# Weight sums of the last stage's fourteen Strassen tiles: from VectorE to GpSimd

## The reference

```python
y = jax.nn.gelu(y).astype(h.dtype)
y = y * jax.nn.sigmoid(y @ w_glu + b_glu)              # w_glu 2048 x 2048
...
xa = memory_attention(xq, mem_n, xa_w_kv[i])           # 4 heads, 256 memory tokens
y = jnp.concatenate([seq_out, xa], axis=-1) * jax.nn.silu(z)
x = x + y @ w_out[i]                                   # w_out 3072 x 1024
return rms_norm_2(x, final_norm_w)
```

## Time and profile before

| | |
|---|---|
| median of 3 runs | 1545.64 us (1544.82 to 1546.47) |
| profiled execution, its own time | 1545.65 us |
| its span, first to last instruction | 1543.7 us |
| mean granted TensorE clock | 0.994 |
| busy: TensorE, VectorE, ScalarE, GpSimd | 97%, 44%, 19%, 12% |
| the last stage | 1345.1 to 1543.7 us of the span |
| GpSimd in the last stage | 2.08 us busy |

### The profile page before, as it was taken

The page is one execution under the profiler, slowest core; times in us unless marked ns, Lnnn a source line. Parts: engine busy times, 40 slices in busy tenths (PEclk is TensorE's granted clock), DMA queues, the critical chain, the costliest instruction groups (busy, mean ns, idle before and its releaser), DMA issues. The chain is left out here.

```text
span 1543.7 us, 22762 instructions
## 1 busy us (share of the span) xinstructions
PE 1496.5 (97%) x9125; PEld 987.0 (64%) x9125; DVE 680.3 (44%) x1313; ACT 293.9 (19%) x559; POOL 184.2 (12%) x161
## 2 busy tenths in 40 slices
PE   6999999999999999999899999999999999999998
PEld 2485655344344344344368688888888888588887
DVE  2444324111111111111624336384479889785663
ACT  2222202111111111111120031100223323230000
POOL 0000000000000000000546620397000000000000
PEclk9999999999999999999999999999999999999999
DMA  9544639899999999999423343455454444424441
GB/s 401 219 164 164 268 130 417 330 421 422 421 422 422 422 422 421 422 422 423 178 110 141 132 149 124 173 215 213 162 186 168 166 144 161 177 110 152 159 163 44
DMA packets 58291, 384.44 MB, mean 249 GB/s; under 512 B 7521, under 2 KB 18529, under 8 KB 23665
## 3 DMA queue, kind: packets, MB, share of 16 engines
q1 hardware_dynamic: 55632, 378.21, 62.0%
q10 hardware_dynamic: 2592, 5.31, 0.9%
HBM read 378.19 MB, written 5.31 MB: 248 GB/s over the span
## 5 line engine op out<-in xcount | busy, mean ns | idle before, releaser
L1247 PE MATMUL ps<-ring,x_gathered 128*64 128x512 f32 x1024 | 227.5, 597 | 0.9 <-DVE x_gathered L1312 0.9
L1321 DVE TENSOR_TENSOR act_slots<-gate,ps 64x512 f32<-64x512 f32 x32 | 22.1, 690 | 380.9 <-ACT gate L1285 380.9
L2386 PE MATMUL ps<-hT,ring 128*128 128x256 f32 x768 | 168.3, 379 | 1.9 <-PEq L116 1.9
L1247 PEld LDWEIGHTS ps<-ring,x_gathered 128*64 128x64 f32 x1024 | 74.1, 138 | 148.3 <-issue 148.3
L2386 PEld LDWEIGHTS ps<-hT,ring 128*128 128x128 f32 x768 | 144.8, 190 | 21.5 <-issue 2.3
L1270 PE MATMUL ps<-ring,act_turned 128*64 128x512 f32 x512 | 116.9, 598 | 0.0
L1270 PEld LDWEIGHTS ps<-ring,act_turned 128*64 128x64 f32 x512 | 33.9, 136 | 79.1 <-issue 54.8
L1225 PE MATMUL ps<-y,selT 64*128 64x512 f32 x264 | 75.0, 634 | 0.7 <-ACT y L1291 0.7
L262 PE MATMUL ps<-ring,hT 128*128 128x512 f32 x160 | 69.8, 593 | 0.0
L1687 PE MATMUL ps<-ring,zT 128*128 128x256 f32 x288 | 67.2, 380 | 2.4 <-DVE glu_by_token L1549 1.3
L1214 PEld LDWEIGHTS ps<-sel,h 128*128 128x128 bf16 x1584 | 48.5, 98 | 29.1 <-issue 26.0
(11 more groups left out here) (647 smaller groups left out, 2424.3 us busy)
## 6 DMA issues: line engine op xcount, KB each, us to landing
ring<-in_experts SPq DMA_DIRECT2D x192, 1024.0 KB, 15.6
ring<-in_weights SPq DMA_DIRECT2D x75, 2048.0 KB, 7.8
s_c_bar<-c_bar_out ACTq DMA_DIRECT2D x16, 256.0 KB, 2.9
c_bar<-s_c_bar SPq DMA_DIRECT2D x16, 256.0 KB, 2.7
b_raw<-in_s_b SPq DMA_DIRECT2D x16, 128.0 KB, 7.1
s_a_rows<-s_ab_rows SPq DMA_DIRECT2D x64, 32.0 KB, 6.3
b_by_state<-in_s_b_by_state SPq DMA_DIRECT2D x16, 128.0 KB, 2.7
x<-in_x ACTq DMA_DIRECT2D x1, 1024.0 KB, 5.1
```

Of the source, the lines that this page charges most:

```text
L1247: last = pe.matmul(h_ps[rows, :], xg[:, f, :], w[:, kk, m, :], start=(f == 0), stop=(f == KD - 1))
L1321: dve.tensor_tensor(act_s[:], gate[:], h_ps[upper, :], ALU.mult).then_inc(act_ready, 1)
L2386: last = pe.matmul(out[:, f, :], w[:, kk, (2 * h + f) * P:(2 * h + f + 1) * P], rhs[:, kk, :], start=(kk == 0), stop=(kk == KD - 1))
```

## The change

`sum_weights` is called with GpSimd instead of VectorE for all fourteen tiles, in one run at the start of GpSimd's stream. A wait for the attention's scores stands before tile 1, since the second set of sum buffers lies over the queries that the scores read. Nothing else is altered: TensorE's, ScalarE's and SyncE's streams stay the same.

```diff
             @block.vector
             def _(dve):
-                glu.sum_weights(dve, 0)
                 dve.wait_ge(y_gelu, 1)
                 glu.dve_rows(dve, 0)
...
                 glu.dve_rows(dve, 1)
-                glu.sum_weights(dve, 1)
                 dve.wait_ge(exp_done, 1)
...
                 out.dve_rows(dve, 0)
-                out.sum_weights(dve, 0)
                 glu.dve_first_banks(dve, 3)
                 glu.dve_last_bank(dve, 3)
-                out.sum_weights(dve, 1)
                 gate(3)
                 out.dve_rows(dve, 1)
-                out.sum_weights(dve, 2)
-                out.sum_weights(dve, 3)
                 out.dve_add(dve, 0)
-                out.sum_weights(dve, 4)
-                out.sum_weights(dve, 5)
...
             @block.gpsimd
             def _(pool):
+                glu.sum_weights(pool, 0)
+                pool.wait_ge(scored, 1)
+                for i in range(1, 8):
+                    glu.sum_weights(pool, i)
+                for i in range(6):
+                    out.sum_weights(pool, i)
                 out.pool_rstd(pool)
```

More of the change, by code:

```diff
@@ L2676, in _ @@
                 last.then_inc(p_ready, 1)
-                glu.sum_weights(dve, 2)
                 glu.dve_first_banks(dve, 0)
@@ L2681, in _ @@
                 glu.dve_last_bank(dve, 0)
-                glu.sum_weights(dve, 3)
                 dve.wait_ge(turned, 1)
                 dve.tensor_copy(pT[:], t_ps[:]).then_inc(pT_ready, 1)
-                glu.sum_weights(dve, 4)
                 glu.dve_first_banks(dve, 1)
                 glu.dve_last_bank(dve, 1)
-                glu.sum_weights(dve, 5)
                 def gate(n):
@@ L2701, in _ @@
                 out.dve_rows(dve, 2)
-                glu.sum_weights(dve, 6)
                 gate(0)
@@ L2706, in _ @@
                 glu.dve_last_bank(dve, 2)
-                glu.sum_weights(dve, 7)
                 gate(2)
                 out.dve_rows(dve, 0)
-                out.sum_weights(dve, 0)
                 glu.dve_first_banks(dve, 3)
                 glu.dve_last_bank(dve, 3)
-                out.sum_weights(dve, 1)
                 gate(3)
                 out.dve_rows(dve, 1)
-                out.sum_weights(dve, 2)
-                out.sum_weights(dve, 3)
                 out.dve_add(dve, 0)
-                out.sum_weights(dve, 4)
-                out.sum_weights(dve, 5)
                 dve.wait_ge(rows_in, 16)
```

## The result

| | before | after |
|---|---|---|
| median | 1545.99 us (4 runs, 1544.82 to 1546.47) | 1556.56 us (4 runs, 1555.15 to 1558.05) |
| ratio | | 1.0064 (95% interval 1.0049 to 1.0079) |
| profiled execution, its time | 1545.65 us | 1555.66 us |
| its span | 1543.7 us | 1553.6 us |

What follows compares the result with a forecast made beforehand. The prediction took TensorE, busy for 97% of the span, as the bound, not VectorE. Its terms, 6.1 + 1.6 + 0.3 = 8.0 us on 1545.65, gave 1553.7 us, with a range of 1549.0 to 1558.0.

Steps and rivals of the forecast that it cites:

- term 1: Start of gate tile 0: GpSimd's weight sums and stretched row sums delay it from 1353.02 to 1359.15, +6.1 us.
- term 2: Before output tile 0: gate 2 and four row sums take turns with GpSimd's sums, +1.6 us.
- term 3: Before output tile 2: gate 3 and its row sums meet that tile's GpSimd sums, +0.3 us.
- rival B: At the stage's start the last row sum gets in before tile 1's first sum: +6.3 us in all, 1551.9; chance 0.20.
- Hidden work: After gate tile 0: later sums, scaling of p and the long product fit behind TensorE's tiles of at least 12.1 us.
- C: Terms 2 and 3 lose more turns, or sums miss a 12.1 us window: 1556 to 1558.5 us; chance 0.18.
- A: The main forecast, all three terms as counted: 1553.7 us; chance 0.50.
- D: Not slower: the engines don't disturb each other where it matters, the gap before output tile 0 closes; 1546.2 us; chance 0.10.
- E: Faster by over 0.2%, which only a change in the tail could bring; chance 0.02.

Runs made afterwards that it cites:

- run with the extra wait: Changed kernel with one more GpSimd wait: gate tile 1's sums start only when the first four row sums are done; 1554.95 us, ratio 1.0056.
- the filler: Changed kernel with unused extra matmuls between the scores and gate tile 0: thirty gave 1560.53 us, ratio 1.0095; fifteen gave 1554.42 us, ratio 1.0038.
- the delay without GpSimd: Kernel before, sums still on VectorE, with five unused VectorE additions ahead of the first row sums and GpSimd idle; 1557.39 us, ratio 1.0075.
- Banks first: Last gate products taken out of PSUM ahead of output tile 1's row sums; tile 0 on VectorE 1544.63 us, kernel before 1544.86, changed kernel 1554.49.

## Why the prediction was right, and what it lacked

**Point by point.** The bound was read rightly: relieving VectorE brought nothing that could be found, and TensorE's idle time at two places set the result. In the profiled executions, whose times differ by 10.0 us and whose spans by 9.9:

| | forecast | measured |
|---|---|---|
| term 1, start of gate tile 0 | +6.1 (1359.15) | +5.9 (1358.94) |
| clock after that idle time | no term | +3.0 |
| term 2, before output tile 0 | +1.6 | +1.0 |
| term 3, before output tile 2 | +0.3 | 0.0 |
| sum | +8.0 | +9.9 |

The range held the result, but the mechanism was not complete: a term of 3.0 us was missing, and terms 2 and 3, 0.9 us too large together, hid some of it. That the forecast came within 3 us of the median is in that part luck, and the upper end of the range, 1558.0, had been set for more lost turns, not for the clock.

*Term 1* held in each step: the third sum ended at 1352.80, the fourth at 1355.55, and the last row sum lost its turn to tile 1's first sum and ended at 1358.84 (forecast 1359.05). The run with the extra wait shows that this turn is worth 2.1 us, so rival B would have been right in its size and wasn't what happened.

*Missing term.* The sum moved tile 0 by 6 us and counted its 12.1 us as before. The forecast held an idle time of 6.6 us in its own numbers and asked what it would delay, but not in what state TensorE would come out of it. That is 3.0 us, nearly a third of the effect; the filler and the delay without GpSimd show that it belongs to the idle time. The Trainium skill has it (TensorE: Matmul & The Clock Gate, "Part 1: The HAM clock gate"): TensorE falls to half rate after it has stood idle. The rows agree: half speed on the first groups behind 6.6 and behind 4.45 us. It should have been a rival with a price, and the price stood in the trace of the kernel before, in the earlier stage:

```profile
790.38 2.75 PE L1592 MATMUL ps<-zT,hT 128*128 128x256 f32 x8 [2.92 <-DVE gla_qk L1630]
792.93 2.86 PE L1592 MATMUL ps<-ring,gla_xqT 128*128 128x256 f32 x8
795.63 1.89 PE L1592 MATMUL ps<-ring,hT 128*128 128x256 f32 x8
```

Behind 2.92 us of idle time the first two groups took 5.25 us there. In the kernel with all but tile 0 on GpSimd the clock stayed up behind the same idle time, and they took 3.55:

```profile
790.82 1.99 PE L1592 MATMUL ps<-zT,hT 128*128 128x256 f32 x8 [2.92 <-DVE gla_qk L1630]
792.65 1.89 PE L1592 MATMUL ps<-ring,gla_xqT 128*128 128x256 f32 x8
794.37 1.89 PE L1592 MATMUL ps<-ring,hT 128*128 128x256 f32 x8
```

*Term 2* was right in kind, too large by 0.6 us. Gate 2 and the GpSimd instruction queued behind it (3.30 us, 0.95 more than alone) ended within 0.1 us of their forecast places behind tile 6's end. Then GpSimd's instructions ended 2.2 us behind the row sum ahead of them, where I had counted 2.4:

```profile
1463.06 2.79 POOL L1468 TENSOR_TENSOR ring<-ring 128x1024 f32<-128x1024 f32 x1
1466.00 2.62 POOL L1470 TENSOR_TENSOR memT<-ring,hT 128x1024 f32<-128x1024 f32 x1
```

```profile
1461.02 2.62 DVE L1484 TENSOR_TENSOR xa_p<-zT 128x512 f32<-128x512 f32 x1
1463.73 2.67 DVE L1486 TENSOR_TENSOR xa_p<-xa_p,zT 128x512 f32<-128x512 f32 x1
1469.09 0.68 DVE L1489 TENSOR_TENSOR zT<-zT 128x512 f32<-128x512 f32 x1
```

The last row sum ended at 1469.77, 12.8 us behind tile 6's end, not 13.1, and output tile 0 followed it by 2.73 us, not 2.9.

*Term 3* was nothing: output tile 1 starts at 1485.56 and tile 2 at 1497.65, 12.09 later. The row sums made it by 0.2 us.

*Hidden work.* The 12.1 us windows held, also where the long product (now L2677, 5.06 us) stood before tile 3's first sum, which took 4.05 us. No gate tile from 1 to 7 waited. The scaling of p, eight instructions, took 2.19 us, since GpSimd was done with tile 1 by then; in the kernel with tile 0 on VectorE it did fall beside GpSimd's sums, and the eight took 8.48.

*Rivals.* C gave a time (1556 to 1558.5) nearer to the median than A's, but by another mechanism: no further turn was lost. D and E are out.

**What stays open.** "Banks first", in the two kernels with tile 0 on VectorE, gives 3.3 to 3.5 us in the medians, but 1.7 in the stage's length. In the profile of the kernel before the clock did not fall in its 1.34 us of idle time; whether it does in other executions, as it did in two of five profiles with 2.4 us, was not seen.

## What to carry to other kernels

Before moving work to an idle engine, look at the first item of a pipeline: in the steady part the slower engine was hidden by 12 us of matmuls, and at the start it was exposed in full. Leave the first tile with the fast engine. Where two engines read SBUF side by side, count in turns, and look at what the slow one starts next: the last short instruction on which TensorE waits can lose its turn to work that nobody needs yet. And where a sum makes TensorE idle for some microseconds, add what its clock costs afterwards, which the groups behind a like idle time in the same trace can show, or look whether a reorder closes the gap: here moving four row sums behind the instructions that TensorE waited for was worth more than moving fourteen tiles.

## What was not expected of the hardware

The clock also fell in a short idle time, and not each time. Behind the same 2.4 us before output tile 0 it stayed at 1.00 in the changed kernel, in the kernel with all but tile 0 on GpSimd and in the one with thirty extra matmuls, and fell in the two others, for 1.7 us. Behind 4.45 and 6.6 us it fell in all five profiles that had them, for 2.4 and 3.0 us. The 2.92 us at 790 us are in all twelve profiles: the clock fell behind them in ten, among them those of the kernel before and of the changed one, and stayed up in the two others, whose stages began earliest (1343.98 and 1343.16). Behind 1.34 us it stayed up in all four that had them. So part of the spread of such a kernel's runs (1555.15 to 1558.05, with mean granted clocks of 0.992 to 0.989) can come from a few short waits; of the changed kernel only one execution was profiled, so this is not shown.
